# A macaron encoder layer on one core: the last quarter of a head's transposes and one convolution tap change places

## What is computed

```python
def one_block(qblk):
    s = jnp.einsum('bqhd,bkhd->bhqk', qblk, k, preferred_element_type=jnp.float32) * scale
    p = jax.nn.softmax(s, axis=-1).astype(v.dtype)
    return jnp.einsum('bhqk,bkhd->bqhd', p, v)
...
a = u[..., :C_CONV] * jax.nn.sigmoid(u[..., C_CONV:])
a = lax.conv_general_dilated(a, conv_w[i], window_strides=(1,),
                             padding=[(CONV_PAD, CONV_PAD)],
                             dimension_numbers=('NWC', 'WIO', 'NWC'),
                             feature_group_count=C_CONV) + conv_b[i]
...
q = (_rms(cq) * g_q_lat[i]) @ w_q_up[i]          # per head 96 columns, then QK-norm and rotary
att = _attention(q, k, v)
mix = jnp.concatenate([a, att], axis=-1) @ w_out[i]
h = h + gm[:, None, :] * mix
```

## Time and profile before

| | us |
|---|---|
| median of 3 runs | 1960.23 |
| lowest and highest | 1959.33, 1962.48 |
| the profiled execution, its own time | 1960.74 |
| its span, first to last instruction | 1958.9 |
| PE busy | 1865.1 (95%) |
| DVE busy | 1362.3 (70%) |
| ACT busy | 794.9 (41%) |
| POOL busy | 769.0 (39%) |
| mean granted clock of PE | 0.981 of 2.4 GHz |

### The profile page before, as it was taken

The page is one execution under the profiler, slowest core; times in us unless marked ns, Lnnn a source line. Parts: engine busy times, 40 slices in busy tenths (PEclk is TensorE's granted clock), DMA queues, the critical chain, the costliest instruction groups (busy, mean ns, idle before and its releaser), DMA issues.

```text
span 1958.9 us, 22748 instructions
## 1 busy us (share of the span) xinstructions
PE 1865.1 (95%) x8034; PEld 1473.2 (75%) x8034; DVE 1362.3 (70%) x1854; ACT 794.9 (41%) x1248; POOL 769.0 (39%) x600
## 2 busy tenths in 40 slices
PE   5999999999999999996999999999999999999997
PEld 4777777778888878985565555878788888888886
DVE  6767777885777785766788877247655555477778
ACT  4632222222344554235676643144322333334453
POOL 1064545456200010017999942013656555620000
PEclk9999999999999999997999999999999999999999
DMA  9055556544773351000000014122323332476333
GB/s 323 31 174 179 187 176 211 193 156 144 249 253 97 97 203 44 28 0 1 1 1 1 0 54 150 44 81 86 103 92 108 102 108 92 138 260 246 97 108 123
DMA packets 134877, 232.12 MB, mean 118 GB/s; under 512 B 8813, under 2 KB 68308, under 8 KB 134515
## 3 DMA queue, kind: packets, MB, share of 16 engines
q1 hardware_dynamic: 134480, 230.69, 34.8%
q10 hardware_dynamic: 290, 0.05, 0.0%
HBM read 177.75 MB, written 52.95 MB: 118 GB/s over the span
## 4 chain that ended last, share of the span: by engine, by line
PE 55%; DVE 16%; POOL 13%; issue 11%; ACT 2%; DMA 2%; ACTq 0%; DVEq 0%; POOLq 0%; SPq 0%
PE ps L491 18%; PE ps L841 18%; PE ps L365 5%; PE ps L2688 4%; POOL sums L450 4%; PE ps L1624 2%; POOL HID L555 2%; PE ps L2599 2%; DVE ring L468 2%; DVE cv L1791 2%; DVE negmax L1561 1%; PE ps L1602 1%; POOL rqk L1712 1%; DVE ada_acc L1010 1%; DVE grow L1640 1%
## 5 line engine op out<-in xcount | busy, mean ns | idle before, releaser
L491 PE MATMUL ps<-T,ring 128*128 128x512 f32 x1920 | 442.3, 389 | 0.0
L491 PEld LDWEIGHTS ps<-T,ring 128*128 128x128 f32 x1920 | 360.7, 188 | 75.4 <-DVE ring L468 0.2
L491 PE MATMUL ps<-B,ring 128*128 128x512 f32 x1440 | 351.7, 401 | 5.0 <-DVE SG L548 4.9
L491 PEld LDWEIGHTS ps<-B,ring 128*128 128x128 f32 x1440 | 275.3, 191 | 72.4 <-issue 14.6
L941 POOL TENSOR_SCALAR stat<-stat 128x1 f32<-128x1 f32 x32 | 9.4, 293 | 547.0 <-ACT XS L866 256.1
L555 POOL TENSOR_TENSOR HID<-HID,SG 128x512 f32<-128x512 f32 x80 | 118.6, 1483 | 255.9 <-DVE HID L540 145.5
L841 PE MATMUL ps<-PW 128*128 128x512 f32 x924 | 218.2, 391 | 0.0
L468 DVE TENSOR_TENSOR ring<-sums,ring 128x512 fp32r<-128x512 f32 x160 | 120.1, 762 | 134.3 <-ACT ring L462 134.3
L841 PE MATMUL ps<-PT 128*128 128x512 f32 x900 | 212.1, 390 | 0.0
L841 PEld LDWEIGHTS ps<-PW 128*128 128x128 f32 x924 | 174.1, 189 | 36.3
L841 PEld LDWEIGHTS ps<-PT 128*128 128x128 f32 x900 | 168.5, 188 | 34.9
(11 more groups left out here) (325 smaller groups left out, 3303.6 us busy)
## 6 DMA issues: line engine op xcount, KB each, us to landing
adat<-ffn_hidden SPq DMA_DIRECT2D x154, 256.0 KB, 2.7
ada_raw<-in_w_ada SPq DMA_DIRECT2D x56, 512.0 KB, 3.7
rawg<-in_ffn_wg SPq DMA_DIRECT2D x22, 1024.0 KB, 5.5
rawu<-in_ffn_wu SPq DMA_DIRECT2D x22, 1024.0 KB, 5.2
ffn_hidden<-HID SPq DMA_DIRECT2D x84, 256.0 KB, 2.0
ffn_hidden<-base SPq DMA_DIRECT2D x66, 256.0 KB, 2.0
H<-in_x SPq DMA_DIRECT2D x16, 512.0 KB, 6.0
h_saved_rows<-H SPq DMA_DIRECT2D x16, 512.0 KB, 2.6
```

Source lines behind the costliest of these rows:

```text
L491: mm = e.matmul(ps[:, product_bank(M, k)], ring[:, place % RING, wx, kc], RIGHT[k][:, xx, kc], start=(kc == 0 and i == 0), stop=(kc == HC ...
```

## The change

The fourth quarter of a head's transposes (n = 3, the last half of its queries) leaves the last quarter of the first unit and stands in the first quarter of the second unit, on PE between `pe_max` and `pe_scores`, on ACT behind `act_pv_copy`, on DVE behind `dve_max`. `pe_max_row` at the end of the first unit asks for three read quarters and no longer four; the moved transposes have a wait for `m_lo` of their own. The tap that DVE had in the first quarter of the second unit goes to the last quarter of the first unit, behind `dve_max_lo` and ahead of `dve_pv_scale`. Nothing is added or removed; the same instructions run in another order. The transposes move in the 7 pairs that have a next head, the tap in the 6 pairs of turns 0 to 2.

```diff
@@ pe_max_row
             ahead = m % NH == 1 and not (isinstance(i, int) and i == TURNS - 1 and m // NH == 1)
-            e.wait_ge(qk_lo, i * 8 + (4 * (m // NH) + (8 if ahead else 4)))
+            e.wait_ge(qk_lo, i * 8 + (4 * (m // NH) + (7 if ahead else 4)))
@@ pe_turn_head
                 if n == 0:
                     e.wait_ge(m_lo, i * 4 + (hp * 2 - 1))
+                elif n == 3:
+                    e.wait_ge(m_lo, i * 4 + hp * 2)
@@ beside run_units
+        HEAD_AT = {(0, 0): 0, (0, 1): 1, (0, 2): 2, (1, 0): 3}
@@ ScalarE's unit
-                    if m % NH == 0 and not (last and m // NH == 1):
-                        act_head_unit(e, *next_head(i, m), p)
+                    if (m % NH, p) in HEAD_AT and not (last and m // NH == 1):
+                        act_head_unit(e, *next_head(i, m), HEAD_AT[m % NH, p])
@@ VectorE's unit
-                    if m % NH == 0:
+                    if (m % NH, p) in HEAD_AT:
                         if not (last and m // NH == 1):
-                            dve_head_unit(e, *next_head(i, m), p)
-                    elif not last:
+                            dve_head_unit(e, *next_head(i, m), HEAD_AT[m % NH, p])
+                    elif m % NH == 1 and not last:
                         dve_tap(e, i * DTT + (DT + m // NH * 2 + p // 2), (p % 2,))
                     if p == 3 and not (last and m == NU - 1):
                         dve_max_lo(e, i, m + 1)
+                    if (m % NH, p) == (0, 3) and not last:
+                        dve_tap(e, i * DTT + (DT + m // NH * 2), (0,))
                     if not (first and m < 2):
                         if p < 3:
                             dve_pv_recip(e, *at(i, m - 1), p)
@@ TensorE's unit
-                    if m % NH == 0 and not (last and m // NH == 1):
+                    if m % NH == 0 and p < 3 and not (last and m // NH == 1):
                         pe_turn_head(e, *next_head(i, m), p)
                     if not (last and m == NU - 1):
                         pe_max(e, i, m + 1, p)
+                    if m % NH == 1 and p == 0 and not (last and m // NH == 1):
+                        pe_turn_head(e, *next_head(i, m), 3)
                     pe_scores(e, i, m, p)
```

## The result

The changed kernel takes 1978.7 us in the median of 7 runs (1968.60 to 1983.45), against 1960.23 before. The ratio is 1.0084, with a 95% interval of 1.0068 to 1.0101: **slower by 16 us** by the ratio, by 18.5 between the medians, where I had forecast 5 slower and left everything above 1972 out. The direction was right, the size was not. The runs fall into two groups, two near 1969 and five from 1975.7 to 1983.5.

What follows compares the result with a forecast made beforehand. PE, busy 95% of the span, was taken as the bound, with only its waits to win. Five pairs at +1.3, turn 0's first pair -0.3 and turn 3's first pair -0.9 gave +5.3: 1965.5 us, range 1957.5 to 1972.

Steps and rivals of the forecast that it cites:

- The row, 1.21 earlier: Row of maxima at the first unit's end goes at 996.54, 1.21 us earlier: 0.43 work moved, 0.78 a wait gone.
- The tap meets POOL: Moved tap, issued about 998.94 in the first unit's last quarter, sits out one POOL addition and runs 1000.19 to 1001.28.
- The scaling loses too: DVE's scaling behind the moved tap loses to POOL's next addition, ending near 1003.0, where it ended at 1000.84 before.
- PE waits: Second unit, first quarter: PE's product waits 2.2 us for ACT's copy behind the scaling, starting at 1003.84, not 1002.38.
- The second unit 1.2 later, and +1.3 for the pair: DVE's next maximum at 1006.45 against 1005.23; with later taps +0.45 to +2.05 us per pair, +1.3 taken, five pairs +6.5.
- The clock: PE's clock halving behind the new 2.2 us wait, 1.3 us more per pair; held as rival (c), outside the sum.
- rival (c): The new wait drops PE to half clock in all five pairs, 1.3 us more each: 1972 us; chance 0.12.
- The first pair, -0.3: First pair of turn 0, with no scaling or product to wait for: gain between 0 and 0.78 us, taken as -0.3.
- The first pair of turn 3, -0.9: Transposes move but no tap: row 1.21 us earlier, transposes cost 0.43, the 0.15 behind the copy goes: -0.9.
- Rival (a): DVE and POOL don't collide at the tap's new place; DVE's next maximum 0.83 us earlier: 1954.9 us; chance 0.14.
- rival (d): The change doesn't free the first unit's row, because the maximum, not the head unit, is late: 1960 us; chance 0.06.
- Rival (b): Tap or scaling wins one meeting with POOL: next maximum -0.1 or 0, total 1958.5 to 1959 us; chance 0.21.

## Why the prediction failed, step by step

Against the prediction's clock, the changed trace stands 5.46 us later (the product at 998.33 for 992.87). By that:

- **The row, 1.21 earlier: right.** Forecast 996.54, measured 996.62.
- **The tap meets POOL: right.** Issued at 999.02 for 998.94, 2.25 us for 2.34.
- **The scaling loses too: right.** Its end at 1002.95 for 1003.0. ACT's product came a little later than I had, so POOL even paused for 0.25 and the tap got through in that pause. That one addition was all it sat out may be luck: in the first pair a tap issued just as close behind an addition, with no pause to come, sat out seven instructions.
- **PE waits: right**, 1.94 us for 2.2; the product at 1003.78 for 1003.84.
- **The second unit 1.2 later, and +1.3 for the pair: right without the clock.** A pair with the clock held full took 36.0, +1.6. Of the later taps one newly sat out an addition (2.29 us) and the last, which had 2.42 before, came through in 1.28: both effects that I had bounded, together.
- **The clock: the first step that failed.** I had it as rival (c) with a chance of 0.12 and 1.3 us a pair. It befell all five pairs, at 1.6. The rows for it were there: the clock had halved behind a wait of 2.31, and I forecast one of 2.2. It belonged into the sum, not among the rivals. That is +8 us of the miss.
- **The first pair, -0.3: the second step that failed.** Measured +6.5 in one execution and -1.8 in the next. I let the tap sit out one POOL instruction, as the earlier trace rows had it, and looked at the first pair only for what waits there, not for how long POOL's run is. In the changed trace the tap sat out seven.
- **The first pair of turn 3, -0.9: right in kind**, -1.5 by the rows: PE's product there (1157.28) waits for nobody.
- Rival (a), the tap that meets nobody, and rival (d), the row not freed, are out. Rival (b), one meeting won, is what happens when the tap is one column wide.

The sum with both terms as measured would be 5 x 3.2, with -1.8 to +6.5 for the first pair and -1.5 for turn 3: 12.7 to 21, around the 18.5 between the medians. The upper end is for executions with the long tap, the lower for those without.

## What to carry to other kernels

Before moving a DVE instruction with two operands in SBUF, look at what POOL does at the *new* time of that place, not at the old one, and ask whether the instruction is followed by one on which a chain hangs; the same tap costs nothing in a gap that DVE has anyway, ahead of the low row, and 16 us between the low row and the scaling. Where an added wait of PE comes near the length that has halved its clock elsewhere in the trace, put the half clock into the sum. A change that pays by moving work earlier may bring its neighbours into a meeting that their old time avoided: try the parts alone.

## What the runs showed of the hardware

- A DVE instruction that meets POOL's may be passed over by more than one of them: 8.95, 8.98 and 8.97 us for a tap that takes 1.3 alone, and 6.39, 6.57 and 6.37 in three other kernels, always until POOL paused. In another execution of the same program it was 1.80.
- Which of POOL's instructions a tap sits out went by when it was issued. I counted the 260 taps between 895 and 1150 us that were issued during a POOL instruction, in all twelve traces. With another POOL instruction right behind, the 38 taps issued 0.11 us or less ahead of the end of the first were all passed over by the second (979.35 in the earlier trace rows, 2.42 us), and of the 99 issued 0.14 to 0.90 ahead 97 got in before it (1002.35 in the earlier trace rows). Taps issued just behind the start of a POOL instruction, with 0.9 us or more of it to come and another right behind, are less plain: the 15 at 0.04 to 0.06 us behind the start sat out that one instruction only, while of the ten at 0.08 to 0.25 eight sat out more, all the long ones among them, and two did not (one of them of 2.03, in the second trace of the changed kernel, 932.29). What decides there is open.
- A tap on one column waited 1.1 us for POOL just as one on 1024 does. The Trainium skill ("SBUF — State Buffer", section "Who interferes with whom") has the order of issue decide who blocks. The tap of 979.35, issued ahead of the addition that passed it, doesn't agree with that, nor does the tap of 925.97, issued ahead of the last six of the seven that passed it, and the measurement decides.
- In the five middle pairs of all three traces of the changed kernel's order (the third is the one where POOL waits in the first pair), a wait of 1.94 to 2.08 us was followed by a half clock, at 1.6 us a pair; with 0.61 us of idle time it stayed full. Needless matmuls in the wait made the pair shorter. Waits of 1.45 to 1.56 in the same stage, nine in the traces of three other kernels, left it full eight times and not in the ninth (the tap behind the scaling, 1121.14). The length of a wait alone doesn't tell: in the first pair of the changed kernel PE's transposes ran at full clock (0.61 us for four, 918.36) right behind a wait of 2.35.
